# Prompt attention and delta rule in 128 by 128 tiles, gated norm moved into the last iterations

## The chip, the cores and the metric

The kernel runs on one core of a Trainium2 chip. The metric is device microseconds (us) of one execution. Before the change three runs took 1685.17, 1687.4 and 1690.0 us, the median is 1687.4.

## The reference

One layer of a hybrid decoder is computed for 512 prompt tokens and 8 sample tokens with the same weights: a gated feed-forward network, a mixer, and a second feed-forward network, with RMS norms before and after each. The mixer projects the normed input once and feeds two branches.

- Forgetting attention, 8 heads of width 64. With `c` the running sum of the log forget values, the prompt's scores are `q.k / 8 + c_q - c_k`, masked causally; a softmax over the keys weights the values. Queries are taken in blocks of 128. The samples attend over 4096 cached rows each, read through a page table.
- Gated delta rule, 4 heads of width 128, in chunks of 64 tokens. With `g` the running sum of log decays within a chunk and `beta` a gate per token:

```
lower = (k*beta) k^T * decay          decay[c,s] = exp(g_c - g_s) for s <= c
u, w  = solve((I + strict lower), [v*beta, k*beta*exp(g)])
v_new = u - w S
o     = (q*exp(g)) S + (q k^T * decay) v_new
S     = S*exp(g_last) + (k*exp(g_last - g))^T v_new
```

The delta rule's output `o` is normed over each head and gated: `rmsnorm(o, g_gdn) * silu(z)`. Both branches are projected, weighted by sigmoid gates, summed and projected once more.

## The kernel before

**Layout.** Features lie on partitions, tokens along the free axis: `T` = 520, in two halves of 260 for products with weights. All big products are done in three parts in float32r: each float32 matrix is split into a rounded high part (a ScalarE copy) and the remainder (a VectorE subtraction), and high*high, low*high, high*low are summed (`block_products`, L133 to L152; splits at L126 and L130). Weights stream from memory in blocks of 128 output columns through `w_raw`, `w_high`, `w_low`, two buffers each.

**Stages.** `ffn(0)` takes until some 448 us. `core` (L466) is the mixer up to the branch outputs. Its first part runs the 44 projection blocks (until some 838 us) and beside them the first sample group's attention, convolutions and sample updates. Its second part is a loop over 32 tiles, written out by hand on every engine (`for t in range(N + 2)`: L1034 ScalarE, L1440 VectorE, L1819 TensorE). A tile is a head and a block of 128 queries, `i` = 0 to 3, with `i + 1` blocks of keys. Then come `gated` (L1843) and `merge` (L1906), each a block of its own that begins when all engines have ended the one before, and `ffn(1)`.

**The loop.** In iteration `t` TensorE issues the scores of tile `t`, one delta rule step, a pair of sample key steps (iterations 0 to 11), the transposes of tile `t-1`'s probabilities, the transposes of the samples' probabilities and a pair of sample value steps (iterations 14 to 32), a second delta rule step and the values of tile `t-2`. VectorE takes the maximum of the scores, ScalarE the exponential with the row sum, VectorE scales the probabilities by the inverse sum (`norm`, L1365), TensorE transposes them, ScalarE copies them from PSUM (`turned`), and `values` (L1701) multiplies. Every engine works its instructions strictly in this order. Where the delta rule's steps stand is set by `step_at` (L500): 57 steps spread over the 68 half iterations: 12 of preparation (spread, raw pairs, turn into token order, for each head), 4 inverses, 21 levels of the triangular inverse, 4 solves, and 16 of the recurrence (state and update for each of 8 chunks). `value_at` (L489) places the sample values.

**Shapes on TensorE.** The score of a tile is three products into one bank (L1687 to L1690):

```
pe.matmul(bank[:, 0:S], proj[lo:lo + 64, Q0 + c, i * P:(i + 1) * P],
          proj[lo:lo + 64, K0 + c, 0:S], start=True, stop=False)
pe.matmul(bank[:, 0:S], sel[0:8, h, :], cum[0:8, 0:S], start=False, stop=False)
pe.matmul(bank[:, S - P:S], ident[:, :], causal[:, :], start=False, stop=True)
```

They use 64, 8 and 128 rows of the array, in float32. `values` uses 64 columns, `spread` (L1715) 4 rows in float32r with high and low parts apart, `state` (L1791) 64 columns, `update` (L1806) 64 rows. The sample products use 32 columns in four column groups side by side.

**Around the loop.** Before the first score TensorE turns the prompt's values to token order and VectorE copies them (L1355). GpSimd makes low parts for the decay and beta rows (L825) and masks the levels (L837). After the loop the samples' sums and outputs follow (L1158 to L1186), then `gated`: squares on ScalarE, sums by a product with ones, logarithm and exponential on ScalarE, products and low parts on VectorE, while SyncE loads `x` back (L1860).

## Time and profile before

| what | value |
|---|---|
| profiled execution | 1685.08 us, its span (first to last instruction) 1683.2 us |
| TensorE matmuls busy | 1574.1 us (94%) |
| TensorE weight loads busy | 1407.5 us (84%), beside the matmuls |
| VectorE busy | 601.4 us (36%) |
| ScalarE busy | 502.1 us (30%) |
| GpSimd busy | 131.7 us (8%) |
| read from memory | 253 MB |

Busy time of matmuls overlaps from one to the next, so what one costs is read from start to start. The granted clock is the share of TensorE's full 2.4 GHz; 0.50 is 1.2 GHz.

### The profile page before, as it was taken

What the parts mean: (1) busy time and instruction counts of PE and PEld (TensorE: products, weight loads), DVE (VectorE), ACT (ScalarE), POOL (GpSimd) and SP (SyncE); (2) the same over time, 40 slices, a digit from 0 to 9 for tenths busy, and PEclk for the clock granted to TensorE, in tenths of its full rate; (3) what the DMA queues carried; (4) which work ended last, traced back from release to release, by engine and by line L of the source; (5) the groups of instructions that cost most, each with busy time, mean ns of one, the idle gap of its engine ahead of it and who ended that gap; (6) DMA issues with size and microseconds to landing.
All of it is one profiled execution on the core that took longest, in us unless ns stands there. A gap on an engine that the chain in (4) does not pass through costs nothing. (4 is left out here: it accounts for less than half of the span.)

```text
span 1683.2 us, 31105 instructions
## 1 busy us (share of the span) xinstructions
PE 1574.1 (94%) x12650; PEld 1407.5 (84%) x12650; DVE 601.4 (36%) x889; ACT 502.1 (30%) x742; POOL 131.7 (8%) x152
## 2 busy tenths in 40 slices
PE   5999998999688999999999999978988999998995
PEld 4999998999577888877856776658978999998995
DVE  3333333121633654132455432335434333332113
ACT  4223222221521355221233223232343322222221
POOL 0000000000152000332100220011000000000000
PEclk8999999999899999999979999998999999999998
DMA  3222223222359978999965456745302222222221
GB/s 105 91 97 87 88 99 106 69 86 76 96 172 376 335 267 298 356 332 361 354 225 192 162 188 212 232 164 165 108 31 88 87 87 95 92 92 86 86 86 51
DMA packets 111866, 268.51 MB, mean 160 GB/s; under 512 B 15389, under 2 KB 15902, under 8 KB 111018
## 3 DMA queue, kind: packets, MB, share of 16 engines
q1 hardware_dynamic: 105514, 244.01, 42.3%
q0 software_dynamic: 6272, 23.34, 3.8%
q8 instruction: 61, 1.00, 0.2%
q14 instruction: 19, 0.16, 0.0%
HBM read 253.04 MB, written 14.26 MB: 159 GB/s over the span
## 5 line engine op out<-in xcount | busy, mean ns | idle before, releaser
L130 DVE TENSOR_TENSOR w_low<-w_raw,w_high 128x1024 fp32r<-128x1024 f32 (+1 forms) x180 | 233.0, 1296 | 766.9 <-ACT w_high L126 766.9
L126 ACT ACTIVATE w_high<-w_raw 128x1024 fp32r<-128x1024 f32 (+1 forms) x180 | 200.6, 1116 | 755.5 <-PE psum L151 726.7
L147 PE MATMUL psum<-h_high,w_high 128*128 128x260 f32 x1408 | 286.0, 284 | 16.4 <-DVE h_low L227 16.4
L151 PE MATMUL psum<-h_high,w_low 128*128 128x260 f32 x1408 | 284.9, 284 | 0.0
L149 PE MATMUL psum<-h_low,w_high 128*128 128x260 f32 x1408 | 284.5, 284 | 0.0
L147 PEld LDWEIGHTS psum<-h_high,w_high 128*128 128x128 f32 x1408 | 218.1, 190 | 18.8 <-issue 14.5
L151 PEld LDWEIGHTS psum<-h_high,w_low 128*128 128x128 f32 x1408 | 218.3, 189 | 0.0
L149 PEld LDWEIGHTS psum<-h_low,w_high 128*128 128x128 f32 x1408 | 217.6, 189 | 0.0
L147 PE MATMUL psum<-a_high,w_high 128*128 128x260 f32 x704 | 146.4, 289 | 10.4 <-DVE a_low L383 10.4
L147 PE MATMUL psum<-mix_h_high,w_high 128*128 128x260 f32 x704 | 147.5, 291 | 6.9 <-DVE mix_h_low L227 6.9
L149 PE MATMUL psum<-a_low,w_high 128*128 128x260 f32 x704 | 143.1, 285 | 0.0
L151 PE MATMUL psum<-a_high,w_low 128*128 128x260 f32 x704 | 143.0, 285 | 0.0
L149 PE MATMUL psum<-mix_h_low,w_high 128*128 128x260 f32 x704 | 142.7, 284 | 0.0
L151 PE MATMUL psum<-mix_h_high,w_low 128*128 128x260 f32 x704 | 142.4, 284 | 0.0
L147 PEld LDWEIGHTS psum<-mix_h_high,w_high 128*128 128x128 f32 x704 | 109.0, 190 | 25.4 <-issue 15.9
L147 PEld LDWEIGHTS psum<-a_high,w_high 128*128 128x128 f32 x704 | 111.0, 191 | 11.5 <-DVE a_low L383 10.8
L149 PEld LDWEIGHTS psum<-a_low,w_high 128*128 128x128 f32 x704 | 110.5, 191 | 0.0
L151 PEld LDWEIGHTS psum<-a_high,w_low 128*128 128x128 f32 x704 | 110.0, 191 | 0.0
L149 PEld LDWEIGHTS psum<-mix_h_low,w_high 128*128 128x128 f32 x704 | 109.6, 190 | 0.0
L151 PEld LDWEIGHTS psum<-mix_h_high,w_low 128*128 128x128 f32 x704 | 109.5, 190 | 0.0
L1527 PE MATMUL psum<-kv_ring,query_blocks 128*32 128x256 f32 x1024 | 69.3, 416 | 13.0 <-DVE query_blocks L1101 7.0
L192 PE MATMUL psum<-sq,ones 128*128 128x260 f32 x192 | 56.5, 442 | 22.3 <-ACT sq L170 12.0
(300 smaller groups left out, 1795.8 us busy)
## 6 DMA issues: line engine op xcount, KB each, us to landing
kv_ring<-in_cache_k SPq DMA_DIRECT2D x256, 256.0 KB, 4.0
kv_ring<-in_cache_v SPq DMA_DIRECT2D x256, 256.0 KB, 3.9
...
```

The costliest lines, as they stand in the source:

```text
L126: act.activation(w_high[:, u, 0:nk, :], w_raw[:, u, 0:nk, :], ACT.Copy).then_inc(high_done, 1)
L130: dve.tensor_tensor(w_low[:, u, 0:nk, :], w_raw[:, u, 0:nk, :], w_high[:, u, 0:nk, :].bitcast(F32), ALU.subtract).then_inc(low_done, 1)
L147: pe.matmul(out[h], w_high[:, u, k, :], high[:, k0 + j, tok[h]], start=s, stop=False)
L149: pe.matmul(out[h], w_high[:, u, k, :], low[:, k0 + j, tok[h]], start=False, stop=False)
L151: mm = pe.matmul(out[h], w_low[:, u, k, :], high[:, k0 + j, tok[h]], start=False, stop=e)
L192: mm = pe.matmul(psum[:, 6 + h, 0:HT], ones[:, :], sq[:, u, h * HT:(h + 1) * HT], start=start, stop=stop)
L1527: mm = pe.matmul(psum[32 * j:32 * j + 32, key_bank[r][g], u * P:(u + 2) * P] .rearrange("p (a k) -> p a k", a=2), qbd[:, c, j, :], ring[:, ...
```

## The change

Scores: the two heads of a pair of 64 rows each get a query tile of 128 rows in which the other head's rows are zero (`qz` for the odd head; in `proj` itself, after the copy, for the even one; VectorE's `queries_apart`). The bias is one float32r product of a 128x128 selector with `cr`, which holds the high part in rows 0 to 7, the low part in rows 32 to 39 and zeros elsewhere; the causal mask is float32r. Values: the turned probabilities are the weights, the 64 columns of values move, and the output lies with queries on partitions. It is scaled there by the inverse of the row sum (`out_scaled`) in place of the probabilities, and after eight tiles turned back by four transposes (`out_turned`). Spread: four float32r products with 128 rows instead of seven. State: 128 columns of weights instead of 64. The steps of the delta rule are spread over 62 half iterations, so that they end in iteration 30, and the sample values end there as well. The gated norm's block is gone: its steps stand in iterations 31 to 33 of the loop, and `x` is loaded back in `merge`. The low parts of decay and beta move from GpSimd to VectorE. New small steps stand beside the projection blocks: `forget_parts` (VectorE, block 10), the rounding of the selector and the causal mask (ScalarE, block 9), the clearing of `cr` (GpSimd).

```diff
 PEAK1 = max(key_at) + 1
-value_at = {PEAK1 + 2 + v * 5 // 4: v for v in range(2 * NG)}
+value_at = {PEAK1 + 2 + v + v // 8: v for v in range(2 * NG)}
 turn_at = {t - 1: v // 2 for t, v in value_at.items() if v % 2 == 0}
...
-    n, places = 2 * t + half, 2 * (N + 2)
+    n, places = 2 * t + half, 2 * (N - 1)
     i = n * len(steps) // places
-    return steps[i] if (n + 1) * len(steps) // places > i else None
+    return steps[i] if n < places and (n + 1) * len(steps) // places > i else None
...
-    sel = sb("head_sel", [68, 8, P], F32, scope)
-    causal = sb("causal", [P, P], F32, scope)
+    sel = sb("head_sel", [P, 8, P], F32R, scope)
+    causal = sb("causal", [P, P], F32R, scope)
...
+    ident_r = over("ident_part", [P, P], F32R, "x", 2816)
+    mask_r = over("mask_part", [P, P], F32R, "x", 2944)
+    S = over("gdn_state", [P, GH, P], F32, "x", 3072)
+    otok = over("fox_out_tok", [P, SEQ], F32, "x", 3584)
+    qz = over("second_query", [P, SEQ], F32, "w_low", 2112)
+    mask = over("chunk_mask", [P, P], F32, "w_low", 2624)
...
                 pool.wait_ge(l_pe, GH + i - 1)
             pool.tensor_tensor(pairs(lo_[i % 2][:, :]), pairs(lt[:, i % GH, :]), over_pairs(lev[:, 1 + i // GH, :]),
                                ALU.mult).then_inc(l_mask, 1)
-            if i == 2:
-                pool.wait_ge(p_act, 3 * GH)
+        def gdn_step(kind, i):
+            if kind == "inverse" and i == 0:
+                pool.wait_ge(stored, 48)
+                pool.wait_ge(levels_in, 32)
+                pool.wait_ge(l_upd, GH)
+                level_part(0)
+                level_part(1)
+            elif kind == "level" and i + 2 < HL:
+                level_part(i + 2)
+            elif kind == "solve" and i == 0:
+                pool.wait_ge(p_dve, 9 * GH)
                 pool.dma_start(hmask1[:, :], a["head_mask"]).then_inc(mask_loaded, 16)
+        for t in range(N + 2):
+            for half in range(2):
+                if step_at(t, half):
+                    gdn_step(*step_at(t, half))
+            if t == N - 1:
+                pool.wait_ge(z_in, 16)
+                pool.wait_ge(c_copy, NCH // 2)
+                pool.wait_ge(o_new, 1)
+                for h in range(GH):
+                    pool.tensor_tensor(zt[:, h, :], zt[:, h, :], cv[:, h, :], ALU.mult).then_inc(z_pool, 1)
     @block.scalar
     def _(act):
...
                 for c in range(2 * n - 40, 2 * n - 38):
                     conv_silu(c)
-        act.activation(gb_high[32:36, :], cum[32:36, :], ACT.Copy)
-        act.activation(gb_high[64:68, :], rows[64:68, 0:SEQ], ACT.Copy).then_inc(parts_high, 1)
-        act.wait_ge(fin, 32)
-        for r in (32, 64):
-            act.activation(sel_r[r:r + 4, :, :], sel[r:r + 4, 0:GH, :], ACT.Copy)
         act.wait_ge(s_stored, 32)
-        act.activation(ident_r[:, :], ident[:, :], ACT.Copy)
+        act.activation(ident_r[:, :], ident[:, :], ACT.Copy).then_inc(ident_done, 1)
+        act.wait_ge(gb_zero, 1)
+        act.activation(gbr[32:36, 0, :], cum[32:36, :], ACT.Copy)
+        act.activation(gbr[64:68, 1, :], cum[64:68, :], ACT.Copy).then_inc(parts_high, 1)
...
         def out(c):
-            act.wait_ge(fo_pe, 8 * c + 8)
+            act.wait_ge(fo_turn, c + 1)
             act.activation(fox_high[:, c, 0:SEQ], psum[:, 2, :], ACT.Copy).then_inc(fo_high, 1)
+        def gated_log(h, n):
+            act.wait_ge(z_sum, n + 1)
+            act.activation(inv4[:, h, 0:SEQ], psum[:, 5 + h % 2, :], ACT.Ln, bias=eps_col[:, 0:1],
+                           scale=1.0 / P).then_inc(z_root, 1)
         for t in range(N + 2):
             if t < N:
...
+            if t % 8 == 2 and t > 8:
+                out(t // 8 - 1)
             if step_at(t, 1):
                 gdn_step(*step_at(t, 1))
-            if t % 8 == 1 and t > 8:
-                out(t // 8 - 1)
-        act.wait_ge(so_copy, R)
-        act.activation(fox_high[:, :, SEQ:T], so[:, :, :], ACT.Copy).then_inc(so_copy, 1)
+            if t == N - 1:
+                act.wait_ge(c_copy, NCH // 2)
+                act.wait_ge(o_new, 1)
+                for h in range(GH):
+                    act.activation(inv4[:, h, :], cv[:, h, :], ACT.Square).then_inc(z_sq, 1)
+                gated_log(0, 0)
+                gated_log(1, 1)
+                act.wait_ge(z_sum, 3)
+                act.activation(inv4[:, :, new], by_head(psum[:, 7, 0:NI]), ACT.Ln, bias=eps_col[:, 0:1],
+                               scale=1.0 / P).then_inc(z_root, 1)
+            if t == N:
+                gated_log(2, 3)
+                gated_log(3, 4)
+                act.wait_ge(z_root, 5)
+                for h in (0, 2):
+                    act.activation(inv4[:, h:h + 2, :], inv4[:, h:h + 2, :], ACT.Exp, scale=-0.5).then_inc(z_inv, 1)
+            if t == N + 1:
+                act.wait_ge(so_copy, R)
+                act.activation(fox_high[:, :, SEQ:T], so[:, :, :], ACT.Copy).then_inc(so_copy, 1)
+                for h in range(GH):
+                    act.wait_ge(z_dve, h + 1)
+                    act.activation(gdn_high[:, h, :], cv[:, h, :], ACT.Copy).then_inc(z_high, 1)
+        out(3)
...
+        def forget_parts():
+            dve.wait_ge(cr_zero, 1)
+            dve.tensor_scalar(cr[0:8, :], cum[0:8, :], -DH ** 0.5, None, ALU.mult).then_inc(cr_high, 1)
+            dve.wait_ge(cr_high, 1)
+            dve.scalar_tensor_tensor(out=cr[32:40, :], in0=cum[0:8, :], scalar=-DH ** 0.5,
+                                     in1=cr[0:8, :].bitcast(F32), op0=ALU.mult,
+                                     op1=ALU.subtract).then_inc(cr_low, 1)
...
+        def queries_apart(c):
+            if c:
+                dve.wait_ge(fs_pe, 8 * c)
+            q = proj[64:128, Q0 + c, 0:SEQ]
+            dve.tensor_copy(qz[64:128, :], q).then_inc(qz_done, 1)
+            dve.wait_ge(qz_done, 2 * c + 2)
+            dve.memset(q, 0.0).then_inc(qz_done, 1)
+        dve.wait_ge(block_used, n0 + NB)
+        dve.memset(qz[0:64, :], 0.0).then_inc(qz_done, 1)
+        queries_apart(0)
+        dve.wait_ge(parts_high, 1)
+        dve.tensor_tensor(gbr[0:4, 0, :], cum[32:36, :], gbr[32:36, 0, :].bitcast(F32),
+                          ALU.subtract).then_inc(parts_low, 1)
+        dve.tensor_tensor(gbr[0:4, 1, :], cum[64:68, :], gbr[64:68, 1, :].bitcast(F32),
+                          ALU.subtract).then_inc(parts_low, 1)
...
-        def norm(t):
-            S = (tiles[t][1] + 1) * P
+        def inverted(t):
             dve.wait_ge(f_exp, t + 1)
-            dve.reciprocal(stat[:, t, 2:3], stat[:, t, 1:2]).then_inc(f_dve, 1)
-            dve.wait_ge(f_dve, 2 * t + 1)
-            dve.tensor_scalar(prb[:, t % 2, 0:S], prb[:, t % 2, 0:S], stat[:, t, 2:3], None,
-                              ALU.mult).then_inc(f_dve, 1)
+            dve.reciprocal(stat[:, t, 2:3], stat[:, t, 1:2]).then_inc(f_rec, 1)
+        def out_scaled(t):
+            h, i = tiles[t]
+            at = slice(i * P + DH * (h % 2), i * P + DH * (h % 2) + DH)
+            dve.wait_ge(fo_pe, t + 1)
+            dve.wait_ge(f_rec, t + 1)
+            if t % 8 == 0 and t:
+                dve.wait_ge(fo_turn, t // 8)
+            dve.tensor_scalar(otok[:, at], psum[:, 2, at], stat[:, t, 2:3], None, ALU.mult).then_inc(f_tok, 1)
         def low(c):
...
             if 1 <= t <= N:
-                norm(t - 1)
+                inverted(t - 1)
             if t < N:
                 peak(t)
+            if t % 8 == 7 and t < N - 1:
+                queries_apart((t + 1) // 8)
             if step_at(t, 0):
                 gdn_step(*step_at(t, 0))
+            if t % 8 == 2 and t > 8:
+                low(t // 8 - 1)
             if t in take_at:
                 take_scores(1, take_at[t])
...
                 gdn_step(*step_at(t, 1))
-            if t % 8 == 1 and t > 8:
-                low(t // 8 - 1)
-        probs_sum(1)
-        masked(1)
-        sample_out(1)
+            if t == N + 1:
+                for h in range(GH):
+                    dve.wait_ge(z_inv, h // 2 + 1)
+                    dve.wait_ge(z_pool, h + 1)
+                    dve.scalar_tensor_tensor(out=cv[:, h, :], in0=zt[:, h, :], scalar=vecs[:, V_GDN:V_GDN + 1],
+                                             in1=inv4[:, h, :], op0=ALU.mult, op1=ALU.mult).then_inc(z_dve, 1)
+            if t >= 2:
+                out_scaled(t - 2)
+            if t == N - 1:
+                probs_sum(1)
+                masked(1)
+            if t == N:
+                sample_out(1)
         dve.wait_ge(so_copy, R + 1)
         dve.tensor_tensor(fox_low[:, :, SEQ:T], so[:, :, :], fox_high[:, :, SEQ:T].bitcast(F32),
                           ALU.subtract).then_inc(so_copy, 1)
+        for h in range(GH):
+            dve.wait_ge(z_high, h + 1)
+            dve.tensor_tensor(gdn_low[:, h, :], cv[:, h, :], gdn_high[:, h, :].bitcast(F32),
+                              ALU.subtract).then_inc(z_low, 1)
+        low(3)
     @block.tensor
...
             h, i = tiles[t]
-            c, lo = h // 2, 64 * (h % 2)
+            c = h // 2
             S = (i + 1) * P
+            if t == 0:
+                pe.wait_ge(cr_low, 1)
+                pe.wait_ge(sel_done, 1)
+                pe.wait_ge(ident_done, 1)
+            if t % 8 == 0:
+                pe.wait_ge(qz_done, 2 * c + 3)
             if t >= 2:
                 pe.wait_ge(ft_copy, t - 1)
             bank = psum[:, t % 2, :]
-            pe.matmul(bank[:, 0:S], proj[lo:lo + 64, Q0 + c, i * P:(i + 1) * P],
-                      proj[lo:lo + 64, K0 + c, 0:S], start=True, stop=False)
-            pe.matmul(bank[:, 0:S], sel[0:8, h, :], cum[0:8, 0:S], start=False, stop=False)
-            pe.matmul(bank[:, S - P:S], ident[:, :], causal[:, :], start=False,
+            q = qz[:, :] if h % 2 else proj[:, Q0 + c, 0:SEQ]
+            pe.matmul(bank[:, 0:S], pr(q, i), proj[:, K0 + c, 0:S], start=True, stop=False)
+            pe.matmul(bank[:, 0:S], sel[:, h, :], cr[:, 0:S], start=False, stop=False)
+            pe.matmul(bank[:, S - P:S], ident_r[:, :], causal[:, :], start=False,
                       stop=True).then_inc(fs_pe, 1)
         def probs_turned(t):
             h, i = tiles[t]
-            pe.wait_ge(f_dve, 2 * t + 2)
+            pe.wait_ge(f_exp, t + 1)
             for j in range(i + 1):
...
             pe.wait_ge(ft_copy, t + 1)
             if t % 8 == 0 and t:
                 pe.wait_ge(fo_low, t // 8)
+            elif t:
+                pe.wait_ge(f_tok, t)
             for j in range(i + 1):
-                mm = pe.matmul(psum[lo:lo + 64, 2, i * P:(i + 1) * P],
-                               vtok[:, j, h * DH:(h + 1) * DH], prt[:, t % 2, j * P:(j + 1) * P],
-                               start=(j == 0), stop=(j == i))
+                mm = pe.matmul(psum[:, 2, at:at + DH], prt[:, t % 2, j * P:(j + 1) * P],
+                               vtok[:, j, h * DH:(h + 1) * DH], start=(j == 0), stop=(j == i))
             mm.then_inc(fo_pe, 1)
+        def out_turned(c):
+            pe.wait_ge(f_tok, 8 * c + 8)
+            for i in range(NQ):
+                mm = pe.transpose(pr(psum[:, 2, :], i), pr(otok[:, :], i), ident[:, :])
+            mm.then_inc(fo_turn, 1)
         def gdn_step(kind, i):
...
                     pe.wait_ge(p_tok, 3 * i)
-                g_i, b_i = sel_r[32:36, i, :], sel_r[64:68, i, :]
-                pe.matmul(psum[:, 5, :], g_i, gb_high[32:36, :], start=True, stop=False)
-                pe.matmul(psum[:, 5, :], g_i, gb_low[32:36, :], start=False, stop=True)
-                pe.matmul(psum[:, 6, :], g_i, gb_high[32:36, :], start=True, stop=False)
-                pe.matmul(psum[:, 6, :], g_i, gb_low[32:36, :], start=False, stop=False)
+                pe.matmul(psum[:, 5, :], sel[:, i, :], gbr[:, 0, :], start=True, stop=True)
+                pe.matmul(psum[:, 6, :], sel[:, i, :], gbr[:, 0, :], start=True, stop=False)
                 pe.matmul(pairs(psum[:, 6, :]), ident_r[:, :], over_pairs(mask_r[:, :]), start=False, stop=True)
-                pe.matmul(psum[:, 7, :], b_i, gb_high[64:68, :], start=True, stop=False)
-                pe.matmul(psum[:, 7, :], b_i, gb_low[64:68, :], start=False, stop=True).then_inc(p_bc, 1)
...
                 for h in range(GH):
-                    mm = pe.matmul(psum[r:r + C, 5, h * P:(h + 1) * P], dm[:, h, tok], S[:, h, :],
-                                   start=True, stop=True)
+                    mm = pe.matmul(pr(psum[:, 5, :], h), pr(dm[:, h, :], p), S[:, h, :], start=True, stop=True)
...
                     mm.then_inc(c_out, 1)
+        def gated_sum(h):
+            pe.wait_ge(z_sq, h + 1)
+            if h >= 2:
+                pe.wait_ge(z_root, h - 1)
+            pe.matmul(psum[:, 5 + h % 2, :], ones[:, :], inv4[:, h, 0:SEQ], start=True,
...
+            if t % 8 == 2 and t > 8:
+                out_turned(t // 8 - 1)
+            if t == N:
+                gated_sum(2)
+                gated_sum(3)
             if step_at(t, 0):
                 gdn_step(*step_at(t, 0))
             if t in key_at:
...
+                pe.wait_ge(c_dve, 2 * NCH + 1)
+                pe.wait_ge(c_copy, NCH // 2)
+                gated_sum(0)
+                gated_sum(1)
+                pe.wait_ge(z_sq, GH)
+                pe.matmul(by_head(psum[:, 7, 0:NI]), ones[:, :], inv4[:, :, new], start=True,
+                          stop=True).then_inc(z_sum, 1)
+            if t == N:
+                out_columns(1)
             if t >= 2:
                 values(t - 2)
-        new_values(1)
-        out_columns(1)
+        out_turned(3)
 count["block"] += NB
...
         for m in range(2, KD):
             load_block(sp, a["w_merge"], m, n0 + m, m % 2, KD)
+        sp.dma_start(x[:, :, :], a["x_spill"]).then_inc(x_back, 16)
...
 for h in range(8):
-sel[h, h] = -DH ** 0.5
+sel[h, h] = sel[32 + h, h] = 1.0
 for h in range(4):
-sel[32 + h, h] = sel[64 + h, h] = 1.0
+sel[64 + h, h] = 1.0
 out["sel"] = sel.reshape(P, 1024)
```

## Rows read from the trace of the kernel before

**Rows 1.** Windows: stretch, length, busy and (instructions) of PE, PEld, DVE, ACT, POOL; clock, DMA share, GB/s

```profile
448.00:845.30 397.30, 377.91 (x3390) 315.16 (x3390) 167.67 (x261) 121.84 (x176) 91.57 (x106) 0.98 0.90 315
845.30:862.90 17.60, 17.55 (x83) 10.38 (x87) 6.13 (x16) 4.57 (x11) 0.00 (x0) 0.52 0.55 191
862.90:886.80 23.90, 23.79 (x172) 13.68 (x164) 14.39 (x31) 8.96 (x23) 0.00 (x0) 0.93 0.75 247
886.80:893.60 6.80, 4.52 (x20) 4.29 (x21) 4.12 (x9) 2.09 (x6) 0.00 (x0) 0.50 0.16 63
893.60:1096.70 203.10, 201.78 (x1512) 138.55 (x1510) 78.48 (x200) 61.78 (x152) 26.15 (x21) 1.00 0.60 199
1096.70:1118.90 22.20, 21.79 (x160) 15.20 (x159) 7.20 (x20) 3.66 (x7) 0.00 (x0) 1.00 0.55 202
1118.90:1141.60 22.70, 7.29 (x25) 5.82 (x24) 9.69 (x19) 14.11 (x21) 6.99 (x8) 0.73 0.27 101
...
820.00:845.00 25.00, 22.70 (x265) 19.34 (x264) 12.38 (x15) 5.79 (x10) 5.21 (x7) 1.00 0.97 337
...
1085.00:1105.00 20.00, 20.00 (x137) 11.34 (x137) 5.92 (x19) 3.69 (x9) 0.00 (x0) 1.00 0.74 248
```

**Rows 2.** Timeline of TensorE, iterations 23 and 24: start us, length, engine, line, operation

```profile
1036.52 1.12 PE L1687 MATMUL psum<-proj 64*128 64x512 f32 x2
1037.58 1.12 PE L1689 MATMUL psum<-cum,head_sel 8*128 8x512 f32 x2
1038.63 0.49 PE L1690 MATMUL psum<-causal,ident 128*128 128x128 f32 x2
1038.95 1.06 PE L1786 MATMUL psum<-proj,inverse_t 128*128 128x128 f32 x8
1039.85 1.06 PE L1788 MATMUL psum<-inverse_t,k_tok 128*128 128x128 f32 x8
...
1044.12 0.65 PE L1708 MATMUL psum<-fox_probs_t,proj 128*64 128x128 f32 x4
1044.70 0.49 PE L1687 MATMUL psum<-proj 64*128 64x128 f32 x2
...
1045.86 1.06 PE L1786 MATMUL psum<-proj,inverse_t 128*128 128x128 f32 x8
```

**Rows 3.** Timeline of TensorE, the spread of head 2

```profile
899.15 0.49 PE L1724 MATMUL psum<-g_beta_high,sel_part 4*128 4x512 f32 x1
...
899.72 0.39 PE L1726 MATMUL psum<-g_beta_high,sel_part 4*128 4x512 f32 x1
899.95 0.38 PE L1727 MATMUL psum<-g_beta_low,sel_part 4*128 4x512 f32 x1
...
901.35 0.87 PE L1708 MATMUL psum<-fox_probs_t,proj 128*64 128x128 f32 x6
```

**Rows 4.** Timeline of TensorE, end of the loop

```profile
1117.80 0.38 PE L1568 MATMUL psum<-ident,value_bc 128*128 128x128 f32 x1
```

**Rows 5.** Timeline of VectorE, start of the loop

```profile
842.81 2.48 DVE L1355 COPY proj<-psum 128x512 f32<-128x512 f32 x4 [1.35 <-PE psum L1675]
```

**Rows 6.** Timeline of all engines, the first head's spread

```profile
854.74 0.60 ACT L985 ACTIVATE exp_g<-psum 128x512 f32<-128x512 f32 x1 [5.11 <-PE psum L1730]
...
856.92 0.68 DVE L1397 TENSOR_TENSOR gdn_tmp<-proj,psum 128x512 f32<-128x512 f32 x1
...
857.65 2.08 PE L1737 MATMUL psum<-gdn_tmp,proj 128*128 128x128 f32 x8
```

**Rows 7.** Timeline of all engines, gated norm and start of merge

```profile
1124.64 2.22 ACT L1865 ACTIVATE inv_rms<-proj 128x520 f32<-128x520 f32 x4 [0.53 <-PEq L598]
...
1126.87 1.28 ACT L1868 ACT_TABLE_LOAD   x1
...
1136.37 2.52 DVE L1902 TENSOR_TENSOR gdn_low<-proj,gdn_high 128x520 fp32r<-128x520 f32 x4
...
1141.62 0.80 PE L147 MATMUL psum<-fox_high,w_high 128*128 128x260 f32 x2 [10.66 <-DVE w_low L130]
```

131 lines of the change are left out of this document (49 added, 82 removed).

## The prediction

> **What bounds the kernel now.** I read the windows first, because the edits touch one stage and the end of it. The columns to read are the stage's length, what the matmuls fill of it, and the granted clock. The attention and delta rule loop begins at 845.3 us. In [rows 1] its four stretches from 845.3 to 1096.7 are filled by TensorE: 17.55 of 17.6 us, 23.79 of 23.9, 4.52 of 6.8 and 201.78 of 203.1. VectorE and ScalarE fill 39% and 30% of the longest one. So the loop is bound by TensorE, and what a matmul costs there is paid in full. Two things stand beside it: the clock is halved (1.2 GHz) from 845.3 to 862.9 and from 886.8 to 893.6, with 3.4 us more in between (0.93 over 23.9 us); and from 1118.9 to 1141.6 TensorE is nearly idle, 7.3 us busy in 22.7, while ScalarE and VectorE do the gated norm one after the other. The timeline of one engine comes next, because busy times overlap for matmuls: what one costs is read from the start of a row to the start of the next one.
>
> **Price of a tile shape.** In [rows 2] eight records of 128x128 weights take 0.90 us when their like follow (1038.95 to 1039.85), 0.112 each. A score of four blocks with 64 rows takes 1.06 us for its product (1036.52 to 1037.58), 1.05 for the bias with 8 rows (to 1038.63) and 0.32 for the causal mask (to 1038.95). A score of one block takes 1.16 us for the three (1044.70 to 1045.86), where six records at 0.112 would be 0.67. The rest is the price of changing the shape: about 0.2 us each time (0.1 until the engine is empty, 0.1 for a weight load that nothing covers). The float32r rows [rows 3] give 0.23 us for 512 columns in one pass (899.72 to 899.95).
>
> **Part 1, scores (32 tiles).** By blocks 1, 2, 3, 4 the product costs 0.42, 0.63, 0.84, 1.06 now (the two ends read, the others between them), the bias the same, the mask 0.32: 7.2 us per head, 57.4 in all. With 128 rows in every tile the product loses its 0.2: 0.22, 0.43, 0.64, 0.86. The float32r bias is one pass and can't be below a weight load: 0.11, 0.12, 0.17, 0.23. The mask is one record, 0.11. That is 3.2 us per head, 25.8 in all. Saved: 31.6 us. No row shows float32r with 128 columns. Its price lies between 0.11 (one record of [rows 2]) and 0.22 (two); I take 0.11, because in [rows 3] float32r takes half the records of float32. The other end is 40 x 0.11 = 4 us more.
>
> **Part 2, values (80 products).** Four records with 64 columns of weights take 0.58 us (1044.12 to 1044.70 in [rows 2]); at 0.112 they are 0.45. So 0.13 goes at the leaving side and 0.1 at the entering side of most of the 32 groups: 32 x 0.22 = 7 us. The new form moves 64 columns instead of 128, which gives nothing more, for 0.112 is already the weight load.
>
> **Part 3, delta rule.** The spread of one head takes 2.20 us (899.15 to 901.35 in [rows 3]) for seven products; four float32r products in one shape are 0.92. 4 x 1.3 = 5.2 us. The eight state products lose one change each, 8 x 0.17 = 1.4 us. The update keeps its 64 rows.
>
> **Part 4, added on TensorE in the loop.** Each of the three output turns inside it is four transposes, 0.44 us, 1.3 together. Sum of parts 1 to 4: 31.6 + 7 + 5.2 + 1.4 - 1.3 = 43.9 us of TensorE's time.
>
> **Part 5, where the loop then ends.** The loop's matmuls run from 845.3 to 1117.8, where the sample's new values follow ([rows 4]): 272.4 us. Less 43.9 this is 228.5. The half clock costs some 12.8 of it now (8.8 in 17.6 us, 1.7 in the 3.4 us, 2.3 of 4.52) and the one long idle 2.3. Bare work after the change is 228.5 - 15.1 = 213.4 us. The compressed steps put all delta rule work and all sample values before iteration 31, so only some 4.0 us of it (the last scores, transposes and values) stand behind the start of that iteration: it starts 209.4 us of bare work after the loop's start.
>
> **Part 6, the start of the loop.** VectorE's four value copies end the wait for the first score now (842.81 + 2.48, [rows 5]). Three instructions for the queries (0.3 to 0.5 us each, by half a 128x512 pass at 0.62) fit before 842.8. The two low parts (0.69 each) wait for ScalarE's high parts, which now wait for GpSimd's clearing; they end near 844.2 in place of 842.8. The first score starts 1.4 us later, at 846.8. The bounds are 0 (all in the idle of VectorE) and 3 us.
>
> **Part 7, waits that faster matmuls uncover.** In the first head's spread the chain is ScalarE's exponential at 854.74 and VectorE's product ending at 857.6 ([rows 6]), 2.9 us, and only then can the pairs start at 857.65. At half clock the next scores covered it. Now 0.5 to 1 us of scores stands there. For the spreads in iterations 0 and 3 I count 2 us each, for the two with a key pair between 0.8 each. The turn waits for three VectorE products (2 us) after the pairs: 1 us in iteration 3, 1.8 in iteration 4 where no key pair is. Solve 0.8, even updates 1.2 (four state updates of 0.28 behind 0.6 of scores and values), the three head pair changes 0.9 (TensorE waits until ScalarE and VectorE took the turned outputs). Sum 11.3, of which 2.3 stands in the old trace already: 9 more. Bounds 3 and 18.
>
> **Part 8, the clock.** At 845.3 to 862.9 it was at 1.2 GHz though the engine was 99.7% busy; the work was 4, 8, 64 rows or 32 columns, and it rose when full 128x128 products came. With full tiles I expect it up earlier by about a third to a half of those 28 us, against which the new idle stands: 12.8 becomes 8, 5 us gained. Bounds: nothing gained and 12 gained.
> The Trainium skill (page "TensorE: Matmul & The Clock Gate", section "What's actually happening") says that the gate opens by how busy the engine has been. By that rule alone padding would not move the clock and these 5 us stay away; the trace does not agree with it as worded, since 17.55 of 17.6 us busy stood at clock 0.52 in [rows 1].
>
> So iteration 31 starts at 846.8 + 209.4 + 8 (clock) + 11.3 (waits) = 1075.5, in place of 1096.7.
>
> **Part 9, the end.** From the start of iteration 31: scores 1.2, maximum 0.8, exponential 0.9, its neighbour's copy 0.6, so squares begin near 3.6 and take 2.2 ([rows 7], L1865). Table load 1.3 (7.2), two logarithms and the samples' (8.7); the last transposes wait for two sums, then copy (10.7), two logarithms (12.0), table load (13.3), exponentials 2.2 (15.5). The last two of four VectorE products end at 17.0, the last copy to high at 18.0, four lows of 0.63 at 19.9, the last fox low at 20.6. From VectorE's last low (1136.37 + 2.52) to the first merge matmul at 1141.62 it is 2.7 us now, and that stays: 23.3. The merge starts at 1098.8 in place of 1141.6: 42.8 us earlier. So the gated norm itself is not hidden much: its chain of ScalarE and VectorE stays nearly whole, only sample output, fox output and attention now lie beside it. Between iteration 31 and the merge 44.9 us become 23.3, mostly because matmul work moved forward out of it.
>
> **Costed at nothing.** Before the loop: one ScalarE copy of 1024 and one of 128 columns (1.4 us), VectorE's forget parts (1.4), a clearing on GpSimd behind the landing of the forget store, 0.24 MB more to load. They lie beside products that fill 377.9 of 397.3 us ([rows 1]); uncovered they cost 3. VectorE's queries of heads 2, 4, 6 (1 us each) stand in an engine that is 39% busy. The reload of x moves on SyncE from the gated stage to behind the last merge weights; the first output weights queue behind its 2.1 MB (some 7 us) and have 8 us until TensorE wants them. Uncovered: 3 us.
>
> **Sum.** The execution took 1685.1 us (span 1683.2, 1.9 around it), the median of the three runs is 1687.4. 1685.1 - 42.8 = 1642.3; I say 1643.
>
> **Rivals.** (a) Waits win: part 7 at its upper end and a clock that falls in them as it did at 886.8 (6.8 us at half speed after one wait). 9 + 5 + 3 us more: 1660. For: steps stand closer, fewer matmuls between them. Against: from 893.6 on only 1.3 us of idle. (b) DMA binds: the sample values now come one pair an iteration from 14 to 30, 2.1 MB each. At 337 GB/s ([rows 1]) a pair takes 6.2 us, at the 248 of 1085 to 1105 8.5. Sixteen at 8.5 are 136 against 124 us of matmuls: 12 us more, 1655. Against: 248 was asked for, not a limit. (c) The clock does not care for full tiles, only for busy time: the 12.8 stay, 5 us more, 1648. For: its second fall, at 886.8, follows a wait; against: the 17.6 us before. This is the rule of the Trainium skill's page cited in part 8. (d) Slower: VectorE now ends each iteration with the scaling of an output, which waits for the values at the end of TensorE's iteration. If thereby every iteration's maximum, exponential, transposes and level updates stood behind TensorE instead of beside it, each would pay 0.9 + 0.9 + 0.6 us, 32 x 2.4 = 77 us less 43: 1719. It decides from 1.3 us an iteration. Against: the transposes of a tile come one iteration after its scores, the values two. (e) Better: waits at 3 and clock up at once, 1630. (f) The saving does not come, since the tile change is not the cause of the 0.2 us: then only passes go (bias and mask, 12 us) and the end, 1665.
>
> **How the numbers follow.** Forecast 0.58, (a) 0.14, (b) 0.08, (c) 0.06, (e) 0.07, (f) 0.04, (d) 0.03. Range 1630 to 1662: it holds the forecast, (b), (c), (e) and most of (a). A change under 0.3% (5 us) is what a measurement can't tell from none. Faster by more 0.96, within it 0.01, slower 0.03.
>
> **What would show it.** Four-block scores from product to the next step 1.2 us in place of 2.43, three or fewer records; values 0.112 a record; a spread 0.92. The first score near 846.8; iteration 31 near 1075; merge near 1099 and 1.3 us table loads inside the loop's end. Wrong if TensorE is idle more than 20 us in the loop, if sample value products wait for kv loads, or if 128-column float32r rows stand 0.2 us apart.

## The result and the profile after

The changed kernel takes 1643.24 us (median of 4 runs, 1641.8 to 1644.67) where the kernel before takes 1687.63 beside it: ratio 0.9737, 95% interval 0.9720 to 0.9754, 44.4 us less. Forecast were 1643 us and a range of 1630 to 1662, so the time was met. On another chip, in a later comparison, the same kernel took 1636.71 against 1682.71, ratio 0.9729 (0.9716 to 0.9742), 46.0 us less. The profiled execution of the first comparison took 1641.8 us, its span is 1640.0 us.

The windows of the changed kernel, to be held against [rows 1]; columns as there:

```profile
852.80:857.00 4.20, 4.18 (x37) 2.05 (x37) 0.44 (x2) 1.74 (x3) 0.00 (x0) 0.59 0.36 137
857.00:900.00 43.00, 33.55 (x312) 25.25 (x315) 31.84 (x69) 18.15 (x48) 0.00 (x0) 1.00 0.68 225
900.00:1075.80 175.80, 174.91 (x1501) 137.04 (x1493) 72.91 (x201) 57.40 (x142) 26.22 (x21) 1.00 0.73 247
1075.80:1098.90 23.10, 11.22 (x61) 7.82 (x59) 11.85 (x28) 16.69 (x26) 6.98 (x8) 0.79 0.06 21
```

What to see: the loop runs from 852.8 to 1075.8 before its last tile's scores, 223.0 us where it was 251.4 (845.3 to 1096.7). At half clock stand 2 x (1 - 0.59) x 4.2 = 3.4 us of it, where 27 us stood. TensorE is idle 9.5 of the 43 us after 857 and full from 900 on. From the last tile to the merge it is 23.1 us, where it was 44.9. DMA is busy 0.73 from 900 on, and no engine has a wait for a load in the loop.

The timeline of TensorE, scores of four blocks and of one, against [rows 2]:

```profile
1019.43 1.08 PE L1809 MATMUL psum<-proj,second_query 128*128 128x512 f32 x2
1019.94 0.79 PE L1810 MATMUL psum<-forget_parts,head_sel 128*128 128x512 f32 x1
1020.57 0.22 PE L1811 MATMUL psum<-causal,ident_part 128*128 128x128 f32 x1
1020.72 1.16 PE L1933 MATMUL psum<-proj 64*128 64x128 f32 x8
...
1025.97 0.61 PE L1831 MATMUL psum<-proj,fox_probs_t 128*128 128x64 f32 x4
1026.42 0.44 PE L1809 MATMUL psum<-proj 128*128 128x128 f32 x2
...
1026.76 0.28 PE L1811 MATMUL psum<-causal,ident_part 128*128 128x128 f32 x1
```

From product to mask a tile of four blocks takes 1.14 us (1019.43 to 1020.57) in place of 2.11, a tile of one 0.34 (1026.42 to 1026.76) in place of about 0.84. Four values take 0.45 (1025.97 to 1026.42) in place of 0.58. The bias alone can't be read from start to start: its row begins 0.51 us behind the product (1019.94), before the product's two records are over (1.08 us by the row). Read the two together.

What TensorE waited for in the whole stretch (us in total, times, longest):

```profile
PE psum L1861 <- DVE gdn_tmp L1495: 6.5, 4, 2.3
...
PE psum L1838 <- DVE fox_out_tok L1469: 4.2, 1, 4.2
PE psum L1869 <- DVE attn_t L1505: 2.2, 2, 1.5
...
PE psum L1851 <- ACT proj L1036: 0.8, 1, 0.8
PE psum L1922 <- ACT inverse L1048: 0.5, 1, 0.5
...
PE psum L1922 <- DVE gdn_state L1535: 0.2, 1, 0.2
```

Inside the loop are L1861 (pairs behind a spread), L1869 (turns), L1851 and L1922: 10.2 us. L1838 waits at the end, behind VectorE's work for the norm.

The end of the stage on all engines, against [rows 7]:

```profile
1079.14 2.21 ACT L1102 ACTIVATE inv_rms<-proj 128x520 f32<-128x520 f32 x4
...
1088.99 2.03 ACT L1113 ACTIVATE inv_rms<-inv_rms 128x1040 f32<-128x1040 f32 x2
1090.09 2.77 DVE L1560 SCALAR_TENSOR_TENSOR proj<-silu_z,vecs,inv_rms 128x520 f32<-128x520 f32 x4 [2.29 <-ACT inv_rms L1113]
...
1095.52 0.68 DVE L1473 TENSOR_TENSOR fox_low<-psum,fox_high 128x512 fp32r<-128x512 f32 x1
...
1098.93 0.80 PE L147 MATMUL psum<-fox_high,w_high 128*128 128x260 f32 x2 [4.70 <-DVE w_low L130]
```

The chain is the one forecast, link by link: squares 3.4 us behind the last tile's first score (1075.77), exponentials 13.2, VectorE's products 14.3, its last low part over at 20.4, merge at 23.2.

### The profile page after: what moved, and what is told of

Read it like the earlier page. It is cut to its first block and busy times, and to the rows that moved or that the text cites. A ratio compares the mean times of both kernels' runs of the same rounds, so it can differ in the third digit from the quotient of the medians.

```text
span 1640.0 us, 31045 instructions
## 1 busy us (share of the span) xinstructions
PE 1525.7 (93%) x12584; PEld 1395.7 (85%) x12584; DVE 602.3 (37%) x902; ACT 500.6 (31%) x741; POOL 131.0 (8%) x152
## 5 line engine op out<-in xcount | busy, mean ns | idle before, releaser
L147 PE MATMUL psum<-h_high,w_high 128*128 128x260 f32 x1408 | 287.0, 285 | 14.9 <-DVE h_low L227 14.9
L147 PEld LDWEIGHTS psum<-a_high,w_high 128*128 128x128 f32 x704 | 111.4, 192 | 11.5 <-DVE a_low L383 10.8
```

The source lines that it names most:

```text
L147: pe.matmul(out[h], w_high[:, u, k, :], high[:, k0 + j, tok[h]], start=s, stop=False)
```

## Experiments

Twelve kernels ran, each in 5 rounds beside the kernel before, in three groups with a chip each: first e_tiles_only, e_own_block, e_score64 and e_bias32; then e_keys_first, e_start, e_small64 and e_best; then e_again, e_spread64, e_state64 and e_best2. The first comparison of the changed kernel stands by itself. For each the table gives the ratio to the kernel before and, from its profile, three distances in us: A from the start of the last projection block to the first score, B on to the first score of iteration 31, C on to the merge's first matmul; and how long B stood at half clock. They are taken from starts of TensorE's rows. Distances don't move when the stage as a whole begins late, and that matters here: in four profiles (the changed kernel's first one, e_tiles_only, e_own_block and e_bias32) the projection ends some 6 us late, and the ratios of these four hold such lateness too, in part or whole (last section).

| kernel | median us | ratio (95%) | A | B | C | half clock in B |
|---|---|---|---|---|---|---|
| before | 1687.6 | 1 | 13.4 | 251.4 | 44.9 | 27 |
| changed, first profile | 1643.2 | 0.9737 (0.9720-0.9754) | 15.0 | 222.9 | 23.2 | 3.4 |
| changed, once more (e_again) | 1636.7 | 0.9729 (0.9716-0.9742) | 15.0 | 225.8 | 23.2 | 10 |
| e_tiles_only | 1654.9 | 0.9809 (0.9790-0.9827) | 15.0 | 214.2 | 43.6 | 7 |
| e_own_block | 1653.9 | 0.9795 (0.9774-0.9815) | 15.0 | 225.6 | 31.7 | 9 |
| e_score64 | 1649.3 | 0.9776 (0.9757-0.9796) | 14.8 | 234.0 | 23.4 | 10 |
| e_bias32 | 1654.7 | 0.9801 (0.9783-0.9819) | 15.0 | 233.3 | 23.8 | 5 |
| e_keys_first | 1634.8 | 0.9713 (0.9699-0.9726) | 15.0 | 223.3 | 23.2 | 6 |
| e_start | 1633.2 | 0.9705 (0.9692-0.9718) | 13.7 | 222.9 | 23.2 | 3.4 |
| e_small64 | 1642.6 | 0.9755 (0.9741-0.9768) | 15.0 | 230.0 | 23.2 | 20 |
| e_spread64 | 1640.3 | 0.9751 (0.9738-0.9764) | 15.0 | 227.8 | 23.2 | 16 |
| e_state64 | 1639.0 | 0.9736 (0.9723-0.9749) | 15.0 | 227.2 | 23.2 | 9 |
| e_best | 1633.2 | 0.9701 (0.9687-0.9714) | 13.7 | 222.3 | 23.0 | 3.4 |
| e_best2 | 1631.5 | 0.9696 (0.9683-0.9709) | 13.7 | 222.3 | 20.7 | 3.4 |

**What each half of the change is worth.** In e_own_block the norm's steps leave the loop and stand in a stage of their own behind it, as before. In e_tiles_only the steps' places go back too:

```
-                n, places = 2 * t + half, 2 * (N - 1)
+                n, places = 2 * t + half, 2 * (N + 2)
...
-            value_at = {PEAK1 + 2 + v + v // 8: v for v in range(2 * NG)}
+            value_at = {PEAK1 + 2 + v * 5 // 4: v for v in range(2 * NG)}
```

> The changed matmuls alone: 128 by 128 tiles, float32r bias, outputs divided by the sums; the delta rule's steps keep the places of the kernel before, the samples' work stays behind the loop, and the gated norm is a stage of its own. Shape theory: the loop's matmuls lose 43.9 us as in parts 1 to 4, and most of the 28 us at half clock go too (about 10 us back), against 5 us of new waits and a start that is 6 us later as in the changed kernel's profile: the merge begins 41 to 45 us earlier than before, time near 1644 us. So nearly the whole gain would be here, and the step places and the norm in the loop together worth under 5 us. Rival (f), tile changes are not the cause: only passes go, 12 us, 1675. Second rival: the places matter more than the tiles, because the loop ends on ScalarE and VectorE: 1655 to 1665.

> The changed kernel with the gated norm as a stage of its own behind the loop, as before; step places stay compressed. From the start of iteration 31 to the merge it is 23.2 us in the changed kernel. With a stage of its own: 7 us until the last values and their low part, 1.5 us between the stages, 22.7 us for the norm as in the kernel before: 31 us, so 8 us slower than the changed kernel, near 1651. Rival 1: the norm's chain is hidden hardly at all, 2 us slower, 1645. Rival 2: the norm in the loop is what brings the gain at the end, 20 us slower, 1663.

The windows of the tiles-only kernel from its last tile to the merge:

```profile
1067.00:1087.00 20.00, 19.59 (x159) 15.28 (x158) 7.75 (x26) 3.06 (x6) 0.00 (x0) 1.00 0.62 223
1087.00:1110.60 23.60, 8.10 (x31) 6.15 (x29) 9.84 (x17) 14.70 (x22) 6.99 (x8) 0.68 0.04 9
```

B + C is 296.3 us before, 257.8 with the tiles alone, 257.3 with the compressed places, 246.1 to 249.0 with the norm in the loop. So the tiles bring 38.5 us. This includes all edits to the products, the float32r bias too, and the clock: 7 us at half speed in place of 27 are 10 of the 38.5. The places bring 0.5: they take 11.9 us out of C (43.6 to 31.7) and put 11.4 into B, for TensorE is as full in the first row above as it is in the loop. Work that TensorE does anyway isn't hidden by moving it. At the same clock it would be 1.5, since e_own_block has 2 us more at half speed. The norm in the loop brings 8.4 us against the profile with nearly the same half clock (257.3 to 249.0), as expected (8); in time, 0.9795 to the first comparison's 0.9737, which has the late projection too, is 10 us, and the loop of that one has 6 us less at half clock, which is 3; 8 lies within the two intervals. The tiles-only expectation said 1644 and that the rest was worth under 5 us; it measured 1654.9. The norm alone is more than that, and the waits in its loop are 13.9 us where 3.6 stood before, 10 new ones and not 5; one of 2.7 us, for VectorE's `fox_low` of the pair before, is in none of the other profiles. Its second rival gave the right time, 1655 to 1665, for the wrong reason: the places aren't what is missing.

The end of the kernel with the norm on its own shows where the 8 us come from:

```profile
1093.69 2.21 ACT L1961 ACTIVATE own_inv_rms<-proj 128x520 f32<-128x520 f32 x4 [1.03 <-PEq L616]
...
1110.52 0.80 PE L147 MATMUL psum<-fox_high,w_high 128*128 128x260 f32 x2 [10.66 <-DVE w_low L130]
```

Squares wait here until attention is over (1093.69, 14.9 us behind the last tile's first score at 1078.79); in the changed kernel they begin 3.4 us behind it. Of these 11.5 us 3 are lost again: squares to merge take 16.8 us here and 19.8 there, where ScalarE and VectorE serve attention in between.

**Shape or partial rows?** The scores' product goes back to 64 rows, and VectorE's `queries_apart` is left out; bias and mask stay at 128.

```
-                        q = qz[:, :] if h % 2 else proj[:, Q0 + c, 0:SEQ]
-                        pe.matmul(bank[:, 0:S], pr(q, i), proj[:, K0 + c, 0:S], start=True, stop=False)
+                        lo = 64 * (h % 2)
+                        pe.matmul(bank[:, 0:S], proj[lo:lo + 64, Q0 + c, i * P:(i + 1) * P],
+                                  proj[lo:lo + 64, K0 + c, 0:S], start=True, stop=False)
```

> The changed kernel with the score products at 64 rows again and without the padded queries; bias and mask as changed. Shape theory: two changes of shape for each of 32 tiles, 0.2 us each, one on the product and one on the bias behind it, though the bias itself has 128 rows: 12.8 us slower than the changed kernel, near 1656; the four-block product takes 1.06 and the bias 0.43 from start to start. Rival, partial rows cost by themselves: only the product is longer, 6.4 us, 1649.5, bias 0.23. Clock: if full rows are what lifts it, the loop's start stays at half clock 10 to 20 us longer than 3.4 us, 5 to 8 us more on top; if not, no change.

TensorE's timeline of that kernel, the same tile of one block, with the values before it:

```profile
1028.35 0.61 PE L1828 MATMUL psum<-proj,fox_probs_t 128*128 128x64 f32 x4
1028.89 0.49 PE L1805 MATMUL psum<-proj 64*128 64x128 f32 x2
...
1029.47 0.27 PE L1808 MATMUL psum<-causal,ident_part 128*128 128x128 f32 x1
```

The values, which are not edited, take 0.54 us (0.45 in the changed kernel), and product to mask 0.58 (0.34). In every tile from the ninth on it is the same 0.09 on the instruction ahead of the product and 0.24 on product and bias: 0.33 a tile, 10.6 in 32, not 12.8, so 0.16 to 0.17 a change and not 0.2. The 0.09 stand on an unedited row. B + C grow by 8.4 us against e_again, which has the same half clock. Of the 2.2 us between, 1.1 come back where the loop waited: its waits are 9.0 us in place of 10.1. The time lies between the theory (12.8 us more) and the rival (6.4), so it doesn't decide between them, and the 0.24 alone could be either. e_spread64, below, decides: there the second of two products with 64 rows is 0.09 us longer to the next start than the same product with 128 rows (863.42 to 863.74, against 863.15 to 863.38 in e_again), and the product behind it, which has 128 rows in both kernels, takes 0.33 in place of 0.24. So what costs is the change of shape, with a share at each side. The clock is as in e_again (10 us at half speed): full rows in the scores don't lift it.

**Float32r.** The bias in float32, still with 128 rows.

```
-                        pe.matmul(bank[:, 0:S], sel[:, h, :], cr[:, 0:S], start=False, stop=False)
+                        pe.matmul(bank[:, 0:S], sel[:, h, :].bitcast(F32), cr[:, 0:S].bitcast(F32), start=False, stop=False)
```

> The changed kernel with the bias in float32 in place of float32r, still 128 rows. By records: one block 0.22, two 0.43, three 0.64, four 0.86 in place of 0.11, 0.12, 0.17, 0.23: 1.5 us a head, 12 us in all, near 1655. Rival: float32r at 128 columns already takes 0.22 and float32 hides under waits, 6 us or less.

```profile
1026.59 1.08 PE L1809 MATMUL psum<-proj,second_query 128*128 128x512 f32 x2
1027.50 1.02 PE L1810 MATMUL psum<-forget_parts,head_sel 128*128 128x512 f32 x2
...
1028.51 1.16 PE L1933 MATMUL psum<-proj 64*128 64x128 f32 x8
```

In TensorE's timeline of this kernel the bias has two records, and the tile of four blocks takes 1.92 us to the next step (1026.59 to 1028.51), 1.29 in the changed kernel (1019.43 to 1020.72). By tiles of 1 to 4 blocks I read 0.12, 0.31, 0.47 and 0.62 us more, 1.5 a head: 12 us on these rows, as expected. In the stage it is less: B + C grow by 10.9 us against the first profile of the changed kernel, 10.3 of them at the same clock, and the two ratios with the late projection in both, 0.9801 against 0.9737, give 10.8. The rival (6 us or less) is out, and that 128 columns of float32r cost 0.11 fits: one block costs 0.12 more in float32, which is one record more.

**The waits of the first ten iterations.** Key pairs are put between a spread and its pairs.

```
-            key_at = {i + 3 * i // 10: KP1 + i for i in range(2 * NG - KP1)}
+            key_at = {t: KP1 + i for i, t in enumerate((0, 1, 2, 3, 4, 5, 6, 9, 10, 11))}
...
+                        if key_first:
+                            key_pair(1, key_at[t])
                         if step_at(t, 0):
                             gdn_step(*step_at(t, 0))
```

> The changed kernel with key pairs moved between the forgets' spread and the pairs of the delta rule: a key pair in each of iterations 0 to 6 and 9 to 11, ahead of the pairs. TensorE's four waits there are 2.35, 1.09, 2.14 and 0.96 us in the changed kernel's profile, 6.5 in all. A key pair is 0.9 us: theory, waits fall to 2.5, and 4 us go: 1639. Rival: the wait moves on, since VectorE's and ScalarE's chain to the pairs is also what the turn and the solve behind them wait for: within 1 us of the changed kernel.

TensorE's waits in it:

```profile
PE psum L1869 <- DVE attn_t L1505: 4.0, 3, 1.9
PE psum L1861 <- DVE gdn_tmp L1495: 2.8, 4, 1.1
PE psum L1809 <- ACT fox_probs_t L1069: 0.8, 1, 0.8
```

The pairs' waits fall from 6.5 to 2.8 us as meant, the turns' rise from 2.2 to 4.0, and scores wait 0.8 where they did not: 3.7 less, 2.6 more. B is 223.3 with 6 us at half clock, 222.9 with 3.4 in the changed kernel's first profile: 0.8 us gained at the same clock, where 4 were expected. The rival was right. What has to be covered is VectorE's chain from spread to turn, not one wait in it.

**The loop's start.** VectorE's value copies go ahead of the low parts.

```
+                    for b in range(NQ):
+                        dve.tensor_copy(vtok[:, b, :], psum[:, b, :]).then_inc(vt_copy, 1)
                     dve.wait_ge(parts_high, 1)
                     dve.tensor_tensor(gbr[0:4, 0, :], cum[32:36, :], gbr[32:36, 0, :].bitcast(F32),
```

> The changed kernel with VectorE's four value copies ahead of the two low parts of the forgets (0.68 us each), at the loop's start. Theory: the first score waits for the copies only, so the loop starts 1.4 us earlier, and the first spread has scores ahead of it: 1.4 us less, 1642. Rival: nothing, as the first spread waits for the low parts and is as late as before. The same profile tells whether the projection's end, 5.8 us later in the changed kernel's one profile than in that of the kernel before (block starts differ from 470 us on), comes again in every kernel with the changed loads, or varies from run to run.

VectorE and then TensorE in the changed kernel:

```profile
848.97 0.68 DVE L1441 TENSOR_TENSOR g_beta_parts<-cum,g_beta_parts 4x512 fp32r<-4x512 f32 x1
...
850.29 2.47 DVE L1448 COPY proj<-psum 128x512 f32<-128x512 f32 x4
852.82 0.49 PE L1809 MATMUL psum<-proj 128*128 128x128 f32 x2 [4.27 <-DVE proj L1448]
```

and in this one:

```profile
841.02 2.48 DVE L1443 COPY proj<-psum 128x512 f32<-128x512 f32 x4
843.54 0.68 DVE L1445 TENSOR_TENSOR g_beta_parts<-cum,g_beta_parts 4x512 fp32r<-4x512 f32 x1
843.56 0.49 PE L1809 MATMUL psum<-proj 128*128 128x128 f32 x2 [2.97 <-DVE proj L1443]
```

TensorE's wait falls from 4.27 to 2.97 us, and A from 15.0 to 13.7: 1.3 us where 1.4 were expected, and nothing of it comes back (B is 222.9, as in the first profile of the changed kernel).

**The small edits and the clock.** State products with 64 columns of weights, and the first two products of a spread with 64 rows: together, then each alone.

```
-                            pe.matmul(psum[:, 5, :], sel[:, i, :], gbr[:, 0, :], start=True, stop=True)
+                            pe.matmul(psum[:, 5, :], sel[0:64, i, :], gbr[0:64, 0, :], start=True, stop=True)
...
-            mm = pe.matmul(pr(psum[:, 5, :], h), pr(dm[:, h, :], p), S[:, h, :], start=True, stop=True)
+            mm = pe.matmul(psum[r:r + C, 5, h * P:(h + 1) * P], dm[:, h, tok], S[:, h, :],
...
```

> The changed kernel with 64 columns of weights in the eight state products and 64 rows in the first two products of each of four spreads. Shape theory: 8 x 0.17 and 4 x 2 x 0.2: 3 us slower, 1646. Rival: these stand beside waits and cost nothing, within 1 us.

> The changed kernel with 64 rows in the first two products of each of the four spreads only. With the state products at 64 columns as well, the loop was 6.9 us longer than in the changed kernel, 3 expected, and 20.4 us of it stood at half clock (3.4 in the changed kernel). If partial rows at the loop's start hold the clock down, the loop again has over 13 us at half clock and takes 4 to 5 us longer. If those were chance or the state's, 3 to 10 us at half clock, and only 4 x 2 x 0.16 = 1.3 us more.

> The changed kernel with 64 columns of weights in the state products only, none of which stands in the first five iterations. Expected 8 x 0.2 to 0.3 = 1.6 to 2.4 us more in the loop, and no more half clock at its start than in the changed kernel (3.4 to 10 us). If this one has 20 us at half clock too, neither shape is the cause of it.

> The changed kernel once more, nothing edited. In its first profile the projection's last block began at 837.8 us, in five other profiles of kernels with the same code up to there it began at 829.8 to 831.8, in three others at 837.6 to 838.1. If that is a property of the single run or of the chip, this profile has 831.8 or 837.8 while the way from the first score to the merge is again 246.1 us; the time is then 1636 to 1643. If the changed loads cause it, it is always 837.8. From first mask to start of the last tile it should be 223.7 as in the first profile, within 1 us, with 3.4 to 10 us of it at half clock depending on where the clock's steps of 3.4 us fall.

The windows of the changed kernel once more (e_again has an empty line more at its head, so its line numbers are one higher):

```profile
845.30:855.60 10.30, 7.91 (x48) 5.10 (x49) 3.35 (x10) 4.00 (x9) 0.00 (x0) 0.67 0.62 195
855.60:859.00 3.40, 3.40 (x26) 3.00 (x29) 1.51 (x4) 0.56 (x2) 0.00 (x0) 0.59 0.65 242
```

and TensorE's wait in the first of them:

```profile
854.84 1.96 PE L1862 MATMUL psum<-gdn_tmp,proj 128*128 128x128 f32 x8 [2.34 <-DVE gdn_tmp L1496]
```

and of the one with 64 rows in the spreads:

```profile
845.70:858.40 12.70, 10.35 (x59) 7.10 (x60) 4.41 (x12) 4.56 (x11) 0.00 (x0) 0.64 0.61 213
...
878.90:885.70 6.80, 4.63 (x20) 4.23 (x20) 4.83 (x12) 1.91 (x6) 0.00 (x0) 0.50 0.59 205
```

State products alone: B is 1.4 us longer than in e_again with nearly the same half clock, what part 3 said of them. Spreads alone: 2.0 us longer, 0.2 on each spread's rows, and a second fall of the clock, 33 us into the loop (0.50 for 6.8 us). The half clock is what was expected (16 us, over 13), the 4 to 5 us longer loop is not: its waits are 0.7 us shorter, the rest isn't followed up. Both together: 4.2 us longer with 20 us at half clock, 10 more than in e_again, which is 5 us; the products of these two edits can't be read from that sum.

In the changed kernels every fall of the clock inside the loop follows a wait of TensorE for over 2 us. In e_again the clock is up 6.2 us after the first score, TensorE waits 2.34 us for the pairs (854.84), and 3.4 us at half clock follow; in the changed kernel's first profile the same wait (2.35) stands and nothing follows. That makes 3.4 and 10 us for the same code. The fall at 33 us follows a wait of 2.13 us, which e_again has too (2.14), without a fall. Both kernels with 64 rows in the spreads show that fall, and none of the other eleven profiles of changed kernels shows one at that place; but e_tiles_only, with 128 rows, has one of the same kind 132 us into the loop, behind a wait of 2.7 us, and the kernel before has one at 886.8 [rows 1]. Before that it has 3.4 us at half clock from 869.8 on with TensorE busy throughout, so there a fall came with no wait at all. So a second fall needs no products with 64 rows. Whether they make it likelier, or only move the wait to where the clock falls, is not settled.

**The end, and a faster version.** e_best takes the orders of e_keys_first and e_start, and in the last iterations puts the last output's scaling and parts ahead of the norm's. e_best2 also takes VectorE's four low parts of the norm out of the stage and puts them behind the merge's first weight split:

```
                     split_low(dve, n0, 0, KD)
+                    for h in range(GH):
+                        dve.tensor_tensor(gdn_low[:, h, :], cv[:, h, :], gdn_high[:, h, :].bitcast(F32),
+                                          ALU.subtract).then_inc(z_low, 1)
                     split_low(dve, n0 + 1, 1, KD)
...
+                                       by_chunk=(z_low, -4) if m == 0 else None)
```

> The changed kernel with the key pairs ahead of the pairs, the value copies ahead of the low parts, and in the last iterations the last attention output and its parts ahead of the gated norm's. If all hold: 4 + 1.4 + 1.5 us less than the changed kernel, 1636. If the end's chain is ScalarE's logarithms and exponentials and not VectorE's order, the last 1.5 stay: 1638. Rival: the end is bound otherwise and waits move on: within 2 us of the changed kernel.

> The kernel with three orders changed (key pairs first, value copies first, attention output ahead of the gated norm's parts), and the four low parts of the gated norm moved behind the merge's first weight split, where the merge's attention half of the first block covers them. In the kernel with the three orders VectorE was busy without a gap to the end of the stage, so its order alone brought 0.2 us. Taking four instructions of 0.63 us out of it should bring the merge's first matmul 2.3 us forward: start of iteration 31 to the merge 20.7 us in place of 22.9. Rival: the products of the second half wait for the low parts, whose place behind the weight split is 1.2 us later, and the 2.3 us come back there: no change in time.

The end in e_best2:

```profile
1084.93 0.69 DVE L1472 TENSOR_TENSOR fox_low<-psum,fox_high 128x512 fp32r<-128x512 f32 x1
1086.12 2.00 ACT L126 ACTIVATE w_high<-w_raw 128x1024 fp32r<-128x1024 f32 x2 [0.35 <-PEq L614]
...
1088.35 2.52 DVE L2044 TENSOR_TENSOR gdn_low<-proj,gdn_high 128x520 fp32r<-128x520 f32 x4
1088.49 0.80 PE L147 MATMUL psum<-fox_high,w_high 128*128 128x260 f32 x2 [6.00 <-DVE w_low L130]
```

In e_best the order alone brings 0.2 us in C, not 1.5: VectorE is busy from its first product (1090.09 in the changed kernel) to its last low part almost without a gap, so the order of its work doesn't matter. The wait of the last transposes falls from 4.2 to 0.4 us and comes back as a longer one for the merge's weights, 8.3 in place of 4.7. Taking work out of the chain does help: C is 20.7, the 2.3 us expected. From its first matmul to the end of the span the merge's side takes 541.2 us in both, so nothing comes back there. e_best2 is the fastest version: 1631.54 us, ratio 0.9696, beside 1636.71 and 0.9729 for the changed kernel on the same chip, 5.2 us less. By the distances 1.3 us of it come from the start and 2.5 from the end; of the 3.5 us in B some 3 are half clock (3.4 in place of 10 us), which I would not count on.

## Why the prediction was right, and where only the sum was

**The bound.** Right. TensorE fills the loop, and the 128 by 128 tiles alone bring 38.5 us from the first score on. The forecast has 39.9 for this: 43.9 of work and 5 of clock less 9 of waits. The sum is near, its terms less so: in e_tiles_only the clock brings 10 and the new waits cost 10.

**Price of a shape.** 0.2 was too much by a fifth as a change that one puts in (0.33 a tile, two changes). Part 1 went from rows, so that it hardly mattered.

**Part 1, scores.** Product, bias and mask of the last 24 tiles sum to 44.0 us before and 20.5 after; for 32 tiles 31.3 saved, 31.6 forecast.

**Part 2, values.** Eight values with their two edges: 1.22 us before (0.20 on the instruction ahead, 0.82 and 0.20), 0.95 after: 0.27 x 32 = 8.6, forecast 7.

**Part 3.** A spread takes 1.03 to 1.13 us where the clock is up, not 0.92; 4.5 saved and not 5.2. The four float32r rows of the changed kernel's spread of head 1 and what follows:

```profile
867.43 0.50 PE L1851 MATMUL psum<-g_beta_parts,head_sel 128*128 128x512 f32 x1
867.76 0.39 PE L1852 MATMUL psum<-g_beta_parts,head_sel 128*128 128x512 f32 x1
...
868.23 0.40 PE L1854 MATMUL psum<-g_beta_parts,head_sel 128*128 128x512 f32 x1
868.56 1.72 PE L1642 MATMUL psum<-kv_ring,query_blocks 128*32 128x256 f32 x28
```

The first and the last step take 0.33 and not 0.23. The last goes over to 32 columns, a change of shape that I had left out; the first follows a causal mask of 128 columns in the same shape, and its 0.1 stays unexplained. It is as long behind a wait of 0.76 us (880.62 to 880.95), so it isn't what stands before it. The state products saved 1.4 us, as forecast.

**Part 6, the start.** 1.6 us later than before (A 15.0 against 13.4), forecast 1.4, and by the mechanism named: the low parts stand ahead of the copies. e_start takes 1.3 of it back.

**Part 7, waits.** 10.2 us, forecast 11.3. Single ones: 2.35 and 2.14 for two spreads (2 forecast), 1.09 and 0.96 for the two others (0.8), turns 0.6 and 1.55 (1 and 1.8), solve 0.5 (0.8), updates 0.2 (1.2), head pairs none (0.9). The forecast took 2.3 us of waits for old ones; the old loop has 3.6 (2.4 for the pairs, 0.5, 0.5 and 0.2), so the new ones are 6.6 and not 9. Not seen beforehand was the third spread's wait of 0.8 us for ScalarE's keys by tokens (L1851).

**Part 8, the clock.** The step with the largest miss. Forecast were 8 us of cost. Half clock of 3.4 us costs 1.7, of 9.6 us (the table's 10) 4.8. The loop is the 228.7 us forecast less 6.3 for the clock in the first profile (3.2 in the second), less 1.1 for waits, and some 1.6 longer in bare work: 222.9 (225.8). Those 1.6 are open. With the old waits of 1.3 us that the bare work of the forecast still holds they are 2.9, though parts 1 to 4 by their rows saved 44.5 and not 43.9. The reason given, that full tiles would bring the clock up, is not borne out for the scores: with 64-row products the start has the same 10 us at half clock. By the rule of the Trainium skill (page "TensorE: Matmul & The Clock Gate", section "What's actually happening") padding alone moves nothing, and with that this run agrees; against it stand the 17.6 busy us at clock 0.52 of the kernel before [rows 1], which no run here explains. So rival (c), by which only busy time counts, was right for the scores and wrong in its number: it left 12.8 us of cost. The change of the products as a whole (e_tiles_only) took the half clock from 27 to 7 us, the kernel before by one profile only; which of them did it is not shown. So this step of the forecast had its sign right, its size too small and a reason that no run bears out. The same section says that one kernel has a different count of slow matmuls from run to run, and the two profiles of the changed kernel show that: 3.4 and 10 us.

**Part 9, the end.** 23.2 us, forecast 23.3, the same in all seven profiles of kernels that leave the scores and the end as changed. But the sentence that the gain there comes mostly from matmul work moved forward misleads: that work (11.9 us) lands in the loop, and in sum it brought 0.5. The norm in the loop brought the 8.4, so the forecast's word that the norm is not hidden much was too low. Its chain did stay whole, 19.8 us from squares to merge, but it starts 11.5 us earlier.

**Costed at nothing.** Borne out: in nine profiles with the changed work before the loop the last projection block begins at 829.8 to 832, as before (831.9), and four more begin at 837.6 to 838.2, which is taken up below. The merge to the end takes 541.1 us, before 541.6: the moved reload of x costs nothing.

**The sum.** The merge began at 1098.93 us, 1098.8 forecast, and this agreement is partly luck: in that profile the projection ended 5.8 us late, and the loop was 5.8 us shorter than forecast. In e_again, without the late projection, it began at 1094.3, 4.5 us before the forecast. The gain was forecast at 44.4 us and measured at 44.4 and 46.0.

**The rivals.** (a) waits stayed in their forecast; (b) no sample value waits for a load; (d) from 900 us on TensorE is busy 174.9 of 175.8 us: VectorE's scaling stands beside TensorE's work; (f) fell by e_score64 and e_tiles_only; (e), waits at 3 us and the clock up at once, was half so: the clock nearly, the waits not.
